# Weights of two experts at once on VectorE, one dot later, in a PEER decoder step

## The chip, the core and the metric

The kernel runs as one program on one core of a Trainium2 chip. The metric is the device time of one execution in microseconds (us). A core has these engines, each with an instruction stream of its own: TensorE (PE, its weight loads are listed as PEld), VectorE (DVE), ScalarE (ACT), GpSimd (POOL) and SyncE (SP), and 16 DMA engines that move data between HBM and the on-chip memory. Engines wait for each other by semaphores that the program counts up and waits on.

## The reference, cut to what matters

Two decoder layers for a prompt of 512 tokens and 8 sample tokens, in float32. Each layer has a token mixer (attention or a short convolution), a PEER expert layer and a small gated addition, with layer norms between. Nearly all of the time is PEER: for every token and each of 8 heads, the 16 best of 16,384 experts are found, and for each chosen expert one row of `u_tab` and one of `v_tab` (1,024 numbers each) are fetched.

```
def block(xt):                                  # 128 tokens
    ...
    top_s, top_p = lax.top_k(cand_s, PEER_TOPK)
    idx = jnp.take_along_axis(cand_i, top_p, axis=-1)
    g = jax.nn.softmax(top_s, axis=-1)          # gates: 128 x 8 x 16
    a = jnp.einsum('td,thkd->thk', xt, u_tab[idx])
    hk = (g * jax.nn.gelu(a, approximate=False)).astype(xt.dtype)
    return jnp.einsum('thk,thkd->td', hk, v_tab[idx])
```

So each expert of each token costs a dot of the token with its u row, a gelu of that dot, a product with the gate, and an addition of the v row weighted by that product.

## The kernel before, in words

Tokens lie on the 128 partitions. The prompt is four tiles of 128 tokens; the 8 sample tokens are a tile of their own. For a prompt tile there are 8 heads x 16 experts = 128 gathers; the sample tile's 8 x 128 expert rows are 8 gathers. A gather is one indirect DMA: POOL gives 128 indices, and each partition receives the 8 KB of its expert, u and v side by side. Both layers together have 1,040 gathers of 1 MB. They land in a ring of slots in the tile `arena`: 9 slots for the first 27 gathers, 11 afterwards.

What is done with a gather, in the order in which a slot passes it (experts are handled in pairs, `q` = 0 to 3 in a group of 8):

1. POOL issues the gather (line 989) when the slot has been released by the semaphore `slot_done`.
2. VectorE forms the dot in one instruction (line 1628, in `two_dots`), first of one expert, then of the other.
3. ScalarE does `two_experts` (line 1150): the gelu of the two dots (1154), a drain, two small products gelu x gate (1157, a copy with the gate as scale, 128x1 each), a drain, and the two row weightings (1164): the v row is scaled in place by its weight, 128x1024 each.
4. TensorE adds the weighted v rows to the accumulator `acc` in PSUM (1870 for prompt tiles, 1867 for the sample tile) and counts up `slot_done`.

The gates of a group of 8 are copied next to the gelus before its first pair (1190 for prompt tiles, 1193 for the sample tile). The last 8 experts of the program are not weighted row by row: ScalarE writes a diagonal matrix of the weights (1168), and TensorE multiplies the v rows by it (1855, the last pair 1842). Ahead of those, the accumulated sum is turned over: ScalarE copies `acc` to `yb` once (1172), and TensorE reads it back in (1833).

All other work (routing of the next tile, projections, norms) is cut into background pieces. A plan spreads them over the steps, one step a pair of experts. At step t TensorE does the pieces of step t; ScalarE and VectorE do the same pieces two steps later (`BEHIND = 2`). On both engines a step is first the background pieces, then the pair. Everything is written out in order in the program, so each engine works through a fixed list.

Of the kernel before, what the change touches and what calls it, by code (L numbers as in the profile page):

```python
# [25 lines left out]
P = 128  # L26
# [560 lines left out]
def build(nc, h0, h0T, consts, panels, ple_rows, keysT, uv0, uv1, cache_k, cache_v, pages, wlam, subg, ln, convw,  # L587
# [3 lines left out]
    with ctx:  # L591
        def sb(name, shape, dt=F32):
            return ctx.enter_context(nc.sbuf_tensor(name, shape, dt))
# [35 lines left out]
        act_w = sb("act_w", [P, 3, 2, GROUP])  # L629
# [161 lines left out]
        g_done = sem("gates_ready")  # L791
# [229 lines left out]
        def _(act):  # L1021
# [128 lines left out]
            def two_experts(G, q):  # L1150

                half, s = G % 2, slice(2 * q, 2 * q + 2)
                act.wait_ge(dot_done, G * GROUP + 2 * q + 2)
                nc.scalar.activation(act_w[:, 1, half, s], dots[:, half, s], ACT.Gelu).then_inc(gelu_done, 1)  # L1154
                act.drain()  # L1155
                for r in range(2 * q, 2 * q + 2):
                    nc.scalar.activation(act_w[:, 2, half, r:r + 1], act_w[:, 1, half, r:r + 1], ACT.Copy,  # L1157
                                         scale=act_w[:, 0, half, r:r + 1])
                act.drain()  # L1159
                for r in range(2 * q, 2 * q + 2):  # L1160
                    e = G * GROUP + r
                    if e < FIRST_BY_ROWS:
                        row = uv[:, slot_of(e), D:2 * D]
                        nc.scalar.activation(row, row, ACT.Copy, scale=act_w[:, 2, half, r:r + 1]).then_inc(weighted, 1)  # L1164
                        continue
                    if e >= FIRST_BY_ROWS + DIAGS:
                        act.wait_ge(slot_done, e - DIAGS + 1)
                    nc.scalar.activation(diag[:, r % DIAGS, :], const("ident"), ACT.Copy,
                                         scale=act_w[:, 2, half, r:r + 1]).then_inc(weighted, 1)
                if G * GROUP + 2 * q == FIRST_BY_ROWS:  # L1170
                    act.wait_ge(slot_done, FIRST_BY_ROWS)
                    nc.scalar.activation(yb[:], acc[:], ACT.Copy).then_inc(turned_over, 1)

            gates5 = gate[:].rearrange("p b h (a r) -> p b h a r", a=2)
            later = []
            for kind, layer, b, lots in steps:
# [6 lines left out]
                for t, G, q, hd, lot in window_pairs(layer, b, lots):  # L1183
# [4 lines left out]
                    if q == 0 and b < TB:  # L1188
                        act.wait_ge(g_done, place(layer, b) * HEADS + hd + 1)
                        nc.scalar.activation(act_w[:, 0, G % 2, :], gates5[:, b, hd, t // 4 % 2, :], ACT.Copy)  # L1190
                    elif q == 0:
                        act.wait_ge(ixs_ready, layer + 1)
                        nc.scalar.activation(act_w[:, 0, G % 2, :], gs8, ACT.Copy)
                    two_experts(G, q)
# [18 lines left out]
        def _(dve):  # L1213
# [307 lines left out]
            def gates(b, hd, unit):  # L1521
# [4 lines left out]
                V.tensor_scalar(gate[:, b, hd, :], r_ex, r_inv, None, ALU.mult).then_inc(g_done, 1)  # L1526
# [95 lines left out]
            def two_dots(G, q, x_rows):  # L1622
                for r in range(2 * q, 2 * q + 2):
                    e = G * GROUP + r
                    dve.wait_ge(gathered[slot_of(e)], 16 * (use_of(e) + 1))
                    if r == 0:
                        dve.wait_ge(gelu_done, G * 4 + 4)
                    V.tensor_tensor_reduce(uv[:, slot_of(e), 0:D], uv[:, slot_of(e), 0:D], x_rows, 1.0, 0.0, ALU.mult, ALU.add,  # L1628
                                           dots[:, G % 2, r:r + 1]).then_inc(dot_done, 1)

            later = []
            for kind, layer, b, lots in steps:
# [6 lines left out]
                for t, G, q, hd, lot in window_pairs(layer, b, lots):  # L1639
# [6 lines left out]
                    two_dots(G, q, h[:, b, :] if b < TB else x_sample[:])  # L1646
# [419 lines left out]
```

## Time and profile before

| | us |
|---|---|
| median of 3 runs | 3227.34 |
| lowest, highest | 3224.31, 3230.1 |
| the profiled execution, its own time | 3227.89 |
| its span in the profile | 3226.0 |
| TensorE busy | 2468.8 (77%) |
| VectorE busy | 2265.2 (70%) |
| ScalarE busy | 2039.5 (63%) |
| POOL busy | 1216.8 (38%) |
| mean DMA rate | 384 GB/s |

The span is the time between the first and the last instruction of the profiled execution; its own time is 1.89 us more. Busy shares are averages over the span. The first 330 us are the first layer's mixer; gathers run from then to the end. The page cuts the span in 40 slices; in nearly all of those behind the first five the 16 DMA engines are busy 90% or more. The granted TensorE clock is on average 0.875 of full speed.

### The profile page before, as it was taken

The numbers are of one execution on the slowest core, as the hardware profiler recorded it, in microseconds if no ns is written. First come the engines' busy times: TensorE is split into PE (matmuls) and PEld (weight loads), VectorE is DVE, ScalarE is ACT, GpSimd is POOL, SyncE is SP. The second block draws the span as 40 slices with busy tenths as digits, with TensorE's granted clock in tenths as the row PEclk, the third lists the DMA queues.
The fourth block names the chain that finished last, engine by engine and source line by source line (L and its number), as shares of the span: only waits on it lengthen the run. The fifth ranks groups of instructions, "written<-read, shape, count | busy, mean of one in ns | idle before, by whom it ended". The sixth has DMA issues, their size and how long they took to land.

```text
span 3226.0 us, 42783 instructions
## 1 busy us (share of the span) xinstructions
PE 2468.8 (77%) x13942; PEld 2068.6 (64%) x13942; DVE 2265.2 (70%) x5832; ACT 2039.5 (63%) x3623; POOL 1216.8 (38%) x1100
## 2 busy tenths in 40 slices
PE   9998777767756768777676987888788565687777
PEld 7766676657655657666665866676576554576665
DVE  0664677777688878776767667667667888669655
ACT  0143556676667876566756796556666676668983
POOL 0100444444444433334434444334443354434441
PEclk9998889989877889898898798999899777767899
DMA  4523999999999999999999899999999999989997
GB/s 182 209 105 133 359 408 420 421 403 422 418 421 421 407 418 421 421 419 420 419 415 412 343 421 421 421 421 421 420 417 421 411 412 421 421 337 421 421 421 297
DMA packets 178158, 1237.18 MB, mean 384 GB/s; under 512 B 19918, under 2 KB 23758, under 8 KB 31632
## 3 DMA queue, kind: packets, MB, share of 16 engines
q0 software_dynamic: 156896, 1115.93, 84.1%
q1 hardware_dynamic: 20896, 117.47, 9.1%
q8 instruction: 111, 1.82, 0.2%
q10 hardware_dynamic: 144, 1.05, 0.1%
q14 instruction: 111, 0.91, 0.1%
HBM read 1227.91 MB, written 6.50 MB: 383 GB/s over the span
## 4 chain that ended last, share of the span: by engine, by line
DMA 42%; PE 25%; DVE 14%; ACT 11%; issue 3%; DVEq 2%; ACTq 2%; POOL 1%; SPq 0%
DMA arena<-in_uv,idx 42%; DVE arena L1628 8%; PE acc L1870 7%; ACT arena L1164 6%; PE bank L1897 5%; PE bank L1671 4%; PE bank L1888 2%; PE bank L1718 2%; PE acc L1867 2%; ACT act_w L1157 1%; ACT L1154 1%; ACT L1148 1%; DVEq L1533 1%; ACTq L1155 1%; ACTq L1159 1%
## 5 line engine op out<-in xcount | busy, mean ns | idle before, releaser
L989 POOL DMA_INDIRECT arena<-in_uv,idx x1024 | 1166.2, 1139 | 1656.2 <-PE acc L1870 1420.8
L1870 PE MATMUL acc<-cst,arena 128*128 128x128 f32 x8128 | 1248.4, 315 | 678.6 <-ACT arena L1164 672.4
L1870 PEld LDWEIGHTS acc<-cst,arena 128*128 128x128 f32 x8128 | 1093.4, 164 | 848.4 <-ACT arena L1164 817.4
L1628 DVE CUSTOM_DVE_ANT_0 arena<-arena,h 128x1024 f32<-128x1024 f32 x1024 | 1231.8, 1222 | 496.6 <-DMA arena<-in_uv,idx 470.7
L1164 ACT ACTIVATE arena<-arena,act_w 128x1024 f32<-128x1024 f32 x1032 | 1130.3, 1142 | 37.2 <-issue 2.1
L1154 ACT ACTIVATE act_w<-dots 128x2 f32<-128x2 f32 x520 | 105.6, 203 | 755.8 <-DVE dots L1628 752.6
L1897 PE MATMUL bank<-hT,panel 128*128 128x264 f32 (+2 forms) x1760 | 413.3, 390 | 3.6 <-DMA panel<-in_panels 1.3
L1897 PEld LDWEIGHTS bank<-hT,panel 128*128 128x128 f32 x1760 | 334.5, 198 | 55.5 <-issue 6.2
L1157 ACT ACTIVATE act_w<-act_w 128x1 f32<-128x1 f32 x1040 | 250.2, 287 | 43.2 <-issue 1.1
L1154 ACT ACT_TABLE_LOAD x130 | 166.8, 1283 | 2.0 <-issue 0.2
L1888 PE MATMUL bank<-panel,qT 128*128 128x256 f32 (+1 forms) x640 | 152.6, 394 | 0.0
L1888 PEld LDWEIGHTS bank<-panel,qT 128*128 128x128 f32 (+1 forms) x640 | 112.0, 181 | 30.0 <-issue 2.8
L1888 PE MATMUL bank<-panel,hT 128*128 128x256 f32 (+1 forms) x448 | 104.0, 386 | 0.0
L1148 ACT ACT_TABLE_LOAD x80 | 102.6, 1283 | 1.4
L1888 PEld LDWEIGHTS bank<-panel,hT 128*128 128x128 f32 (+1 forms) x448 | 71.2, 164 | 24.8 <-issue 4.3
L1628 DVE DVE_READ_ACCUMULATOR2_ANT dots<- 128x1 f32 x1040 | 86.1, 83 | 0.0
L1033 ACT ACTIVATE qT<-bank 128x520 f32<-128x520 f32 x16 | 9.7, 604 | 111.9 <-PE bank L1671 111.9
L1462 DVE COPY yb<-tp 128x256 f32<-128x256 f32 x80 | 33.6, 420 | 55.8 <-PE tp L1818 54.6
L1064 ACT ACTIVATE arena<-arena,small 128x128 f32<-128x128 f32 (+3 forms) x64 | 35.5, 556 | 49.6 <-DVE small L1317 49.5
L1671 PE MATMUL bank<-keys,panel 128*128 128x256 f32 x256 | 60.2, 390 | 6.8 <-DMA panel<-in_panels 6.8
L1507 DVE TENSOR_TENSOR yb<-ya,cst 128x512 f32<-128x512 f32 x80 | 55.5, 693 | 12.4 <-issue 1.1
L1818 PE MATMUL tp<-keys,qT 128*128 128x128 f32 (+1 forms) x320 | 57.0, 308 | 7.9 <-issue 7.3
(241 smaller groups left out, 2398.6 us busy)
## 6 DMA issues: line engine op xcount, KB each, us to landing
panel<-in_panels SPq DMA_DIRECT2D x94, 1024.0 KB
arena<-in_uv,idx POOLq DMA_INDIRECT x1024
arena<-in_cache_k POOLq DMA_DIRECT2D x16, 512.0 KB, 5.6
arena<-in_cache_v POOLq DMA_DIRECT2D x16, 512.0 KB, 5.0
arena<-in_panels SPq DMA_DIRECT2D x6, 1024.0 KB, 6.9
arena<-out_y_s POOLq DMA_DIRECT2D x8, 512.0 KB, 5.7
h<-in_h SPq DMA_DIRECT2D x1, 2048.0 KB
out_nv_p<-arena POOLq DMA_DIRECT2D x4, 512.0 KB, 2.9
```

What stands on the lines that cost most here:

```text
L989: nc.gpsimd.indirect_dma_start(uv[:, slot_of(e), :], None, uv_dram[layer], bass.IndirectOffsetOnAxis(ids[:, r:r + 1], 0)).then_inc(gathere ...
L1148: nc.scalar.activation(r_ex, r_tv, ACT.Exp, bias=r_nm, accum_out=r_sum).then_inc(gexp_done, 1)
L1154: nc.scalar.activation(act_w[:, 1, half, s], dots[:, half, s], ACT.Gelu).then_inc(gelu_done, 1)
L1157: nc.scalar.activation(act_w[:, 2, half, r:r + 1], act_w[:, 1, half, r:r + 1], ACT.Copy, scale=act_w[:, 0, half, r:r + 1])
L1164: nc.scalar.activation(row, row, ACT.Copy, scale=act_w[:, 2, half, r:r + 1]).then_inc(weighted, 1)
L1628: V.tensor_tensor_reduce(uv[:, slot_of(e), 0:D], uv[:, slot_of(e), 0:D], x_rows, 1.0, 0.0, ALU.mult, ALU.add, dots[:, G % 2, r:r + 1]).the ...
L1671: m = mm(pj[n % 2][:, PW + G_OFF[g]:PW + G_OFF[g] + G_W[g]], w[:, c, :], src[g][:, c, 0:G_W[g]], start=(c == 0), stop=(c == C - 1))
L1718: t = mm(product_of[0:m, 0:PW], src[group_of(x.b)][:, c, local(x.b):local(x.b) + m], w[:, c, :], start=(c == 0), stop=(c == C - 1))
L1867: m = mm(acc[:, c * P:c * P + NS], row, const("group_of")[:, 0:NS], start=False, stop=True, skip_group_check=True)
L1870: m = mm(acc[:, c * P:(c + 1) * P], row, const("ident"), is_transpose=True, start=False, stop=True, skip_group_check=True)
L1888: last = mm(bank[0:m, x.n % BANKS, 0:PW], src[:, c, local(x.b):local(x.b) + m], weights[:, c, :], start=(c == 0), stop=(c == chunks - 1))
L1897: last = mm(bank[:, x.n % BANKS, 0:width], w[:, c, :], hT[:, c, lo:lo + width], start=(c == 0), stop=(c == C - 1))
```

## The change: who forms the weights, and when

ScalarE's `two_experts` is split in two. `two_gelus` does the gelu only and `two_rows` the two row weightings. The product gelu x gate is formed by VectorE, for two experts with one instruction (`two_weights`, a 128x2 tensor_tensor), straight from the tile `gate`. ScalarE's 1,040 single products, the 130 copies of gates and the two drains of each pair are gone. VectorE does the product of pair t-1 after the first dot of pair t. ScalarE's step is now: background pieces of the step, `two_rows` of the pair before, `two_gelus` of this pair. After a tile's last step, the last pair's product and rows follow directly. The semaphore that told ScalarE of the gates is replaced by one, `gated`, that counts products.

```
-            def two_experts(G, q):
+            def two_gelus(G, q):
                 half, s = G % 2, slice(2 * q, 2 * q + 2)
                 act.wait_ge(dot_done, G * GROUP + 2 * q + 2)
-                nc.scalar.activation(act_w[:, 1, half, s], dots[:, half, s], ACT.Gelu).then_inc(gelu_done, 1)
-                act.drain()
-                for r in range(2 * q, 2 * q + 2):
-                    nc.scalar.activation(act_w[:, 2, half, r:r + 1], act_w[:, 1, half, r:r + 1], ACT.Copy,
-                                         scale=act_w[:, 0, half, r:r + 1])
-                act.drain()
+                nc.scalar.activation(act_w[:, 0, half, s], dots[:, half, s], ACT.Gelu).then_inc(gelu_done, 1)
+
+            def two_rows(G, q):
+                half = G % 2
+                act.wait_ge(gated, G * 4 + q + 1)
                 for r in range(2 * q, 2 * q + 2):
...
@@ ScalarE's step
                         for x in later.pop(0):
                             background(x)
-                    if q == 0 and b < TB:
-                        act.wait_ge(g_done, place(layer, b) * HEADS + hd + 1)
-                        nc.scalar.activation(act_w[:, 0, G % 2, :], gates5[:, b, hd, t // 4 % 2, :], ACT.Copy)
-                    elif q == 0:
-                        act.wait_ge(ixs_ready, layer + 1)
-                        nc.scalar.activation(act_w[:, 0, G % 2, :], gs8, ACT.Copy)
-                    two_experts(G, q)
+                    if t > 0:
+                        two_rows(first_group(layer, b) + (t - 1) // 4, (t - 1) % 4)
+                    two_gelus(G, q)
+                two_rows(G, q)
...
@@ VectorE
+            def two_weights(layer, b, t):
+                G, q = first_group(layer, b) + t // 4, t % 4
+                s = slice(2 * q, 2 * q + 2)
+                dve.wait_ge(gelu_done, SEED_GELU + G * 4 + q + 1)
+                of = gate[:, b, t // 8, t % 8 * 2:t % 8 * 2 + 2] if b < TB else gs8[:, s]
+                V.tensor_tensor(act_w[:, 1, G % 2, s], act_w[:, 0, G % 2, s], of, ALU.mult).then_inc(gated, 1)
...
-                    two_dots(G, q, h[:, b, :] if b < TB else x_sample[:])
+                    x_rows = h[:, b, :] if b < TB else x_sample[:]
+                    dot(G * GROUP + 2 * q, x_rows)
+                    if t > 0:
+                        two_weights(layer, b, t - 1)
+                    dot(G * GROUP + 2 * q + 1, x_rows)
+                two_weights(layer, b, t)
```

VectorE, two steps in the middle of a tile, before. `ISA` is the dot (with the instruction behind it that reads out the sum), the rest are background pieces of the routing.

```order
L1628 ISA arena,dots<-arena,h 128x1024 [waits gathered1]
L1628 ISA dots 128x1
L1628 ISA arena,dots<-arena,h 128x1024 [waits gathered2]
L1628 ISA dots 128x1
L1476 MAX ya<-yb 128x8 x2
```

The same place after.

```order
L1624 ISA arena,dots<-arena,h 128x1024 [waits gathered1]
L1624 ISA dots 128x1
L1633 TENSOR_TENSOR act_w<-act_w,gate 128x2 [waits gelu_done]
L1624 ISA arena,dots<-arena,h 128x1024 [waits gathered2]
L1624 ISA dots 128x1
L1472 MAX ya<-yb 128x8 x2
```

Between the two dots of a pair there is now a product that waits for ScalarE's gelu of the pair before.

ScalarE, steps three and four of the first tile, before. `L1092` and `L1037` are background pieces (they square and spread the sample rows).

```order
L1154 ACTIVATE act_w<-dots 128x2 [waits dots_done]
L1157 ACTIVATE act_w<-act_w 128x1 x2
L1164 ACTIVATE arena<-arena,act_w 128x1024 x2
L1092 ACTIVATE arena<-bank 128x8x4 [waits bank_full]
L1037 ACTIVATE hT<-arena 128x2x132 x4
L1037 ACTIVATE x_sample<-arena 128x264 x3
L1037 ACTIVATE z<-arena 128x264
L1154 ACTIVATE act_w<-dots 128x2 [waits dots_done]
```

The same place after.

```order
L1154 ACTIVATE act_w<-dots 128x2 [waits dots_done]
L1092 ACTIVATE arena<-bank 128x8x4 [waits bank_full]
L1037 ACTIVATE hT<-arena 128x2x132 x4
L1037 ACTIVATE x_sample<-arena 128x264 x3
L1037 ACTIVATE z<-arena 128x264
L1164 ACTIVATE arena<-arena,act_w 128x1024 [waits weights_of_two_experts_ready]
L1164 ACTIVATE arena<-arena,act_w 128x1024
L1154 ACTIVATE act_w<-dots 128x2 [waits dots_done]
```

The row weightings of a pair have moved behind the next step's background pieces.

ScalarE at the end of the program, around the first pair of the last 8 experts, before.

```order
L1154 ACTIVATE act_w<-dots 128x2 [waits dots_done]
L1157 ACTIVATE act_w<-act_w 128x1 x2
L1168 ACTIVATE diag<-cst,act_w 128x128 x2
L1172 ACTIVATE yb<-acc 128x1024 [waits slots_done]
L1154 ACTIVATE act_w<-dots 128x2 [waits dots_done]
```

The same place after.

```order
L1154 ACTIVATE act_w<-dots 128x2 [waits dots_done]
L1168 ACTIVATE diag<-cst,act_w 128x128 [waits weights_of_two_experts_ready]
L1168 ACTIVATE diag<-cst,act_w 128x128
L1172 ACTIVATE yb<-acc 128x1024 [waits slots_done]
L1154 ACTIVATE act_w<-dots 128x2 [waits dots_done]
```

The diagonals, and with them the copy of `acc` behind them, now wait for a product that stands behind the first dot of the following pair.

## Rows read from the trace of the kernel before

**Rows 1.** Busy time by stretch: engines, PEclk, DMA share, GB/s.
```profile
core 0: us, PE busy (x) PEld busy (x) DVE busy (x) ACT busy (x) POOL busy (x), PEclk, DMA share, GB/s
328.00:500.00 172.00, 133.50 (x813) 116.13 (x812) 116.64 (x301) 104.78 (x195) 71.47 (x63) 0.88 0.96 389
...
1000.00:1500.00 500.00, 376.77 (x2222) 327.17 (x2223) 387.05 (x1038) 343.65 (x581) 195.82 (x176) 0.89 1.01 418
...
2780.00:2900.00 120.00, 91.28 (x468) 80.22 (x468) 81.76 (x204) 74.11 (x130) 45.32 (x40) 0.67 0.91 365
...
3170.00:3226.00 56.00, 46.06 (x162) 28.41 (x160) 23.27 (x43) 15.52 (x37) 0.94 (x1) 0.91 0.62 242
```
**Rows 2.** Waits: engine, line <- releaser: us in total, times, longest.
```profile
POOL arena L989 <- PE acc L1870: 1441.3, 574, 13.1
...
DVE arena L1628 <- DMA arena<-in_uv,idx: 470.7, 386, 3.8
```
**Rows 3.** Issue to landing: chain pieces (start, us, what), and a load of 512 KB.
```profile
339.73 9.45 DMA arena<-in_uv,idx
...
2779.05 20.02 DMA arena<-in_uv,idx
...
arena<-in_cache_k POOLq DMA_DIRECT2D x16, 512.0 KB, 5.6
```
**Rows 4.** VectorE in order of time, a steady stretch: start, us, [idle before <-releaser].
```profile
1525.36 1.23 DVE L1628 CUSTOM_DVE_ANT_0 arena<-arena,h 128x1024 f32<-128x1024 f32 x1 [1.25 <-DMA arena<-in_uv,idx]
```
**Rows 5.** VectorE in order of time, 2502 to 2520.
```profile
2508.73 1.23 DVE L1628 CUSTOM_DVE_ANT_0 arena<-arena,h 128x1024 f32<-128x1024 f32 x1 [0.37 <-DMA arena<-in_uv,idx]
...
2512.18 1.23 DVE L1628 CUSTOM_DVE_ANT_0 arena<-arena,h 128x1024 f32<-128x1024 f32 x1 [2.22 <-DMA arena<-in_uv,idx]
```
**Rows 6.** Instruction queue, packets, MB, share: whole span, then 1523:1524, then 2509:2510.
```profile
q14 instruction: 111, 0.91, 0.1%
...
q14 instruction: 1, 0.01, 1.9%
...
q14 instruction: 1, 0.01, 2.0%
```
**Rows 7.** Small VectorE instructions, groups by line: busy, mean ns, idle before.
```profile
L1499 DVE TENSOR_SCALAR ya<-ya 128x16 uint32<-128x16 uint32 x80 | 14.4, 180 | 6.1
L1495 DVE TENSOR_SCALAR ya<-ya 128x1 f32<-128x1 f32 x80 | 10.8, 135 | 0.0
```
**Rows 8.** ScalarE's products, the page's group.
```profile
L1157 ACT ACTIVATE act_w<-act_w 128x1 f32<-128x1 f32 x1040 | 250.2, 287 | 43.2 <-issue 1.1
```
**Rows 9.** ScalarE in order of time in the first tile.
```profile
350.47 0.20 ACT L1154 ACTIVATE act_w<-dots 128x2 f32<-128x2 f32 x1 [1.95 <-DVE dots L1628]
...
351.31 2.19 ACT L1164 ACTIVATE arena<-arena,act_w 128x1024 f32<-128x1024 f32 x2
```
**Rows 10.** Busy time by stretch at the start (columns as rows 1).
```profile
390.00:400.00 10.00, 9.27 (x38) 7.26 (x37) 3.64 (x7) 2.81 (x7) 0.70 (x1) 0.66 0.65 264
...
340.00:440.00 100.00, 74.11 (x448) 64.66 (x448) 61.85 (x140) 64.79 (x119) 39.08 (x35) 0.85 0.95 380
```
**Rows 11.** The two sample tiles: chain, then ScalarE and TensorE in order of time.
```profile
1774.06 25.66 PE acc L1867 x128
...
2844.58 1.06 ACT L1122 ACTIVATE h<-bank 128x512 f32<-128x512 f32 x2
...
2845.21 2.07 PE L1932 MATMUL bank<-lng,cst 8*128 8x512 f32 x2 [1.25 <-ACT h L1122]
```
**Rows 12.** The end: all engines in order of time, then the chain's last add.
```profile
3178.65 1.23 DVE L1628 CUSTOM_DVE_ANT_0 arena<-arena,h 128x1024 f32<-128x1024 f32 x1 [0.23 <-DMA arena<-in_uv,idx]
3178.88 1.00 ACT L1172 ACTIVATE yb<-acc 128x1024 f32<-128x1024 f32 x1
...
3179.93 1.10 PE L1833 MATMUL acc<-cst,yb 128*128 128x128 f32 x8
...
3197.07 3.65 PE acc L1842 x8
```

More of the change, by code:

```diff
@@ L628, in build @@
         dots = sb("dots", [P, 2, GROUP])
-        act_w = sb("act_w", [P, 3, 2, GROUP])
+        act_w = sb("act_w", [P, 2, 2, GROUP])
         small = sb("small", [P, 64])
@@ L790, in build @@
         idx_done = sem("expert_ids")
-        g_done = sem("gates_ready")
+        gated = sem("weights_of_two_experts_ready")
         gathered = [sem(f"gathered{r}") for r in range(SLOTS_UV)]
@@ L1163, in two_experts @@
                         row = uv[:, slot_of(e), D:2 * D]
-                        nc.scalar.activation(row, row, ACT.Copy, scale=act_w[:, 2, half, r:r + 1]).then_inc(weighted, 1)
+                        nc.scalar.activation(row, row, ACT.Copy, scale=act_w[:, 1, half, r:r + 1]).then_inc(weighted, 1)
                         continue
@@ L1168, in two_experts @@
                     nc.scalar.activation(diag[:, r % DIAGS, :], const("ident"), ACT.Copy,
-                                         scale=act_w[:, 2, half, r:r + 1]).then_inc(weighted, 1)
+                                         scale=act_w[:, 1, half, r:r + 1]).then_inc(weighted, 1)
                 if G * GROUP + 2 * q == FIRST_BY_ROWS:
@@ L1172, in two_experts @@
                     nc.scalar.activation(yb[:], acc[:], ACT.Copy).then_inc(turned_over, 1)
-            gates5 = gate[:].rearrange("p b h (a r) -> p b h a r", a=2)
             later = []
@@ L1525, in gates @@
                 dve.drain()
-                V.tensor_scalar(gate[:, b, hd, :], r_ex, r_inv, None, ALU.mult).then_inc(g_done, 1)
+                V.tensor_scalar(gate[:, b, hd, :], r_ex, r_inv, None, ALU.mult)
             def background(x):
@@ L1620, in background, with dot @@
                             gates(x.b, x.hd, x.u)
[L1622 to L1629, printed above, removed]
+            def dot(e, x_rows):
+                G, r = e // GROUP, e % GROUP
+                dve.wait_ge(gathered[slot_of(e)], 16 * (use_of(e) + 1))
+                if r == 0:
+                    dve.wait_ge(gelu_done, G * 4 + 4)
+                V.tensor_tensor_reduce(uv[:, slot_of(e), 0:D], uv[:, slot_of(e), 0:D], x_rows, 1.0, 0.0, ALU.mult, ALU.add,
+                                       dots[:, G % 2, r:r + 1]).then_inc(dot_done, 1)
+            def two_weights(layer, b, t):
[4 more added lines that the diff above has]
+                V.tensor_tensor(act_w[:, 1, G % 2, s], act_w[:, 0, G % 2, s], of, ALU.mult).then_inc(gated, 1)
             later = []
```

## The prediction

> **What bounds the kernel now.** I first read busy time by stretch [rows 1]. From about 330 us on the DMA share stands at 1.01 and the rate at 418 GB/s; it is lower only in the first 110 us of gathering (0.96 over 328 to 500), around the sample tile of the second layer (0.91) and at the end (0.62). No engine is as full: in 1000 to 1500 VectorE has 387 of 500 us, TensorE 377, ScalarE 344. So over some 2,800 us the transfer of expert rows sets the pace, and the engines only have to keep up.
>
> The waits say the same [rows 2]. VectorE's dots wait 470.7 us for gathers to land. POOL waits 1441.3 us for a slot, but that wait costs nothing: a gather of 1 MB takes 2.49 us at the full rate (a dot of 1.23 us behind a wait of 1.25 us, again and again [rows 4]), yet from issue to landing it takes 20 us in the bulk, against 5.6 us for a load with nothing queued ahead of it [rows 3]. The difference, some 14 us, is time in the queue. A slot released 3 or 5 us later there makes its gather wait less in the queue and land at the same time. At the start the cushion is thin: 9.45 us to landing, so about 4 us.
>
> Then I looked for what makes a landing late although the queue is full. In 2502 to 2520 dots start at 2508.73 and 2512.18: 3.45 us apart instead of 2.49, with 2.22 us of waiting for the DMA [rows 5]. In 2509 to 2510 lies a packet of the queue q14, which fetches instructions [rows 6]. 0.91 MB in 111 packets is 8.2 kB each. I counted the trace's records: VectorE 8,109, ScalarE 4,742, POOL 1,341, SP 144, together 112 times 128, so one packet brings 128 instructions. Packets that come when VectorE has gone through a further 128 instructions are followed by such a gap, 8 of 8 times between 2509 and 2811 us. One that belongs to ScalarE, at 1523 us, leaves the pace at 2.48 us [rows 4, 6]. The reading: a gather is whole only when each of the 16 DMA engines has done its share, one of the 16 is always the last, and it is the one that also fetches for VectorE. Each such fetch costs the bound resource 3.45 - 2.49 = 0.96 us.
>
> The Trainium skill speaks against that (Runtime: NRT & Kernel Launch, Instruction fetch mechanics): blocks of 16 KiB are fetched by the sequencer's own DMA queue, a cost "mostly hidden". The trace has packets of 8.2 kB, and the gap behind VectorE's is there; by the page the first term below would be nothing. That is rival A.
>
> **The change part by part.** All terms are made against the profiled execution, 3227.89 us (span 3226.0 and 1.89 around it).
>
> *Removed from ScalarE.* 1,040 products at 287 ns by their rows, or 0.24 us each back to back, 250.2 us [rows 8], the gate copies and 1,040 drains. In the bulk ScalarE is 69% busy [rows 1] and beside the DMA, so this gives nothing there. ScalarE's program is 2,208 instructions shorter, 17 fetches, which by rows 4 and 6 lay on another DMA engine: nothing (if on the bound one, -16 us: rival D).
>
> *Added to VectorE: busy time.* No 128x2 tensor_tensor stands in this trace. The nearest rows are 135 ns for 128x1 and 180 ns for 128x16 [rows 7]; up to the 287 ns of ScalarE's product it could be. At 150 ns, 520 of them are 78 us. They lie within the 470.7 us that VectorE waits for gathers [rows 2]: 0. Were that cover gone (as it is where background pieces crowd), it would be 0.15 us a pair. The product's wait for the gelu is for a pair whose dots ended at least one landing (2.49 us) earlier; the gelu takes 0.20 us, so it is normally long done. It isn't if ScalarE is behind, in two row weightings (2.19 us) and a background piece; behind the product then stand the second dot and all background pieces of VectorE, and behind these TensorE's routing work. In the bulk that is within 14 us of cushion.
>
> *Added to VectorE: instructions.* 520 more are 520/128 = 4.06 fetches at 0.96 us: +3.9. Bounds 0 (hidden) and +3.9.
>
> *Moved: the release of slots.* The rows of a pair are weighted after the next pair's first dot and ScalarE's next background piece, so 2.5 to some 6 us later. In the bulk hidden by the cushion [rows 3]: 0. Four places have little or none.
>
> The start, 340 to 440 us. The DMA share is 0.95 there, against 1.01: 5.9 us of idle DMA, most in 390 to 400 (0.65) [rows 10]; over 328 to 500 it is 0.96, 8.5 us [rows 1]. Two effects oppose each other. From gelu to rows there are 0.84 us (350.47 to 351.31), of which only the gelu's 0.20 and the switch stay [rows 9], so each pair takes ScalarE 0.6 us less where it is nearly full, and its background pieces, which feed the next tile's routing, come before the rows. Against that the slots come free later, with 4 us of cushion. The bounds are -5.9 (all of the idle recovered) and +4 (the 6 us of a late release less the gain of three pairs); I take -2, nearer to the relief, since it acts on every pair and the delay only on those behind a long piece.
>
> The first layer's sample tile, about 1774 us: TensorE is busy without a break for 25.66 us with 128 small adds [rows 11], and that sets the dip. It starts when ScalarE's first rows are done, at most 0.7 us later or earlier: 0.
>
> The second layer's, about 2845 us: TensorE waits 1.25 us for ScalarE's copy `L1122`, which stands behind two row weightings of 2.19 us [rows 11]. Now the copy is a background piece ahead of them, but the last pair of the tile before waits about 1 us longer for its product. Between -1.5 and +1, I take -0.5.
>
> The end. The products of experts 1032 and 1033 now wait for the dot of 1034, which starts at 3178.65 and ends at 3179.88. Then come the product with its signal (0.3), the two diagonals (0.69 us together) and the copy of `acc` (1.00), which before started at 3178.88 [rows 12]. So the copy ends about 3181.9 and TensorE's 1833, at 3179.93 before, starts at about 3181.95. From there to 3200.7 TensorE has no break (the adds, with projections between, up to the last at 3197.07, 3.65 us [rows 12]), while the last gather's dot ends at about 3192.3. So the whole is late: +2.0 (bounds 0, if the planned pieces in between give, and +2.5).
>
> **Sum.** +3.9 - 2.0 - 0.5 + 2.0 = +3.4 us on 3227.89: 3231.3. The median of the runs is 0.55 us below the profiled one, so 3230.7, in round figures 3231.
>
> **The rivals.**
> A: VectorE's fetches cost nothing more (the queue absorbs them, or the last of the 16 DMA engines isn't the one). For: fetches that ScalarE makes show no gap. Against: the gap of 0.96 us behind VectorE's. The sum is then -0.5: 3227.4 - 0.5, about 3227.
> B, slower by more: the loop at the start. A pair's product waits for the landing of the next pair's first gather, so a slot's release now depends on a gather issued later. With 9 slots and 4 us of cushion [rows 3], each pair behind a long ScalarE or VectorE piece holds back two slots, and the idle of 340 to 440 grows by as much again: +5.9 where I took -2, so 3231 + 8 = 3239. It decides as soon as releases come over 4 us later. For it: the share dips to 0.65 already [rows 10]. Against: 64.79 us busy of 100 for ScalarE and 61.85 for VectorE, so a delay is caught up.
> C, faster: the relief of ScalarE at the start wins back the idle by all of 8.5 us [rows 1]: 3231 - 6.5 = 3224 to 3225; with fetches hidden too, 3221.
> D: ScalarE's 17 fetches do lie on the bound DMA engine: -16 beside the rest, with 0.96 us apiece, and the tail's +2.0: 3211 to 3215. The row at 1523 speaks against it. That the change doesn't do what it says is excluded by the order of instructions.
>
> **How the numbers follow.** What a measurement of this kernel can tell from no change is 0.2%, 6.5 us: below 3220.9 is faster, above 3233.8 slower. The forecast of +3.4 has 0.43, with 3227 to 3235 as its own range: 0.31 of it is no change, 0.12 slower. A has 0.22: 0.21 no change, 0.01 faster. B has 0.22: 0.18 slower, 0.04 no change. C has 0.10, one half faster and one half no change. D has 0.03, faster. Together faster 0.09, same 0.61, slower 0.30. The range reaches from C's 3222 to a bit beyond B, 3243 (a second tile's start hit by the same loop).
>
> **What the profile after would show.** If the steps are right: the bulk keeps DMA share 1.01 and 417 to 421 GB/s, but each stretch of 500 us has nearly one VectorE fetch more, and the gaps of about 3.45 us between dots stand behind these; the dots in mid-program come 1 to 3 us later than before against their place at 500 us. The product takes 0.13 to 0.18 us and its waits are mostly absent. In 340 to 440 the DMA share is 0.96 or 0.97. TensorE's 1833 starts 3.2 us behind the dot of expert 1034, instead of 1.3. The forecast is wrong if the share in 340 to 440 falls under 0.93 (B), if the last dots come no later than before relative to the start though 4 fetches were added (A), or if ScalarE's rows are waited for by VectorE in the bulk.

## The result and the profile after

The kernel after takes 3233.03 us (median of 17 runs, 3228.45 to 3236.11), the one before in the same sessions 3227.73 (17 runs). The ratio is 1.0015, with a 95% interval of 1.0008 to 1.0021: some 4.8 us slower (2.6 to 6.8), where +3.4 was forecast. The profiled execution has a span of 3230.8 us, 4.8 more than before.

Busy time by stretch in the profile after (columns as in [rows 1]); the last row is beside [rows 10].

```profile
328.00:500.00 172.00, 134.52 (x799) 114.03 (x798) 119.30 (x329) 88.67 (x130) 73.17 (x63) 0.86 0.95 384
...
1000.00:1500.00 500.00, 383.35 (x2208) 335.92 (x2207) 392.46 (x1123) 294.19 (x382) 209.28 (x177) 0.87 1.00 413
...
2780.00:2900.00 120.00, 90.60 (x482) 78.73 (x480) 84.60 (x225) 63.49 (x84) 46.70 (x43) 0.73 0.96 382
...
3170.00:3226.00 56.00, 47.10 (x184) 28.92 (x185) 26.34 (x53) 15.95 (x29) 4.03 (x4) 0.97 0.66 264
...
340.00:440.00 100.00, 75.84 (x445) 64.32 (x438) 63.04 (x151) 54.05 (x80) 39.95 (x35) 0.81 0.92 368
```

ScalarE is 49 us of 500 less busy in mid-program (294 against 344) and nothing comes of it: the DMA share stays at 1.00 to 1.01. In 340 to 440 the share fell from 0.95 to 0.92 where a rise to 0.96 or 0.97 was forecast; that is under the 0.93 which the prediction had named as a sign of rival B. Around the second sample tile it rose from 0.91 to 0.96.

The waits after (engine, line, releaser: us in total, times, longest).

```profile
POOL arena L989 <- PE acc L1879: 1426.1, 612, 12.1
ACT arena L1164 <- DVE act_w L1633: 975.5, 460, 6.7
...
DVE arena L1624 <- DMA arena<-in_uv,idx: 435.0, 358, 4.0
```

ScalarE's idle time moved from the gelus to the rows: its wait for dots is now a wait for products. VectorE waits 435.0 us for gathers, 36 less than in [rows 2], since the products fill part of it. The product itself, from the page's groups:

```profile
L1633 DVE TENSOR_TENSOR act_w<-act_w,gate 128x2 f32<-128x2 f32 x512 | 80.1, 156 | 53.7 <-ACT act_w L1154 51.1
```

156 ns each, between the bounds of [rows 7], and 51.1 us of waiting for gelus in all.

VectorE's dots in a steady stretch, and the instruction packet in 2475 to 2476.

```profile
2473.36 1.22 DVE L1624 CUSTOM_DVE_ANT_0 arena<-arena,h 128x1024 f32<-128x1024 f32 x1
...
2475.66 1.23 DVE L1624 CUSTOM_DVE_ANT_0 arena<-arena,h 128x1024 f32<-128x1024 f32 x1 [1.07 <-DMA arena<-in_uv,idx]
...
2476.81 0.16 DVE L1633 TENSOR_TENSOR act_w<-act_w,gate 128x2 f32<-128x2 f32 x1
...
2479.11 1.22 DVE L1624 CUSTOM_DVE_ANT_0 arena<-arena,h 128x1024 f32<-128x1024 f32 x1 [2.14 <-DMA arena<-in_uv,idx]
```
```profile
q14 instruction: 1, 0.01, 2.0%
```

As in [rows 5], the dot behind a VectorE fetch comes 3.45 us after the one ahead of it, not 2.49. I took the landing of each gather from the trace and looked, between 500 and 2780 us, at the landings around each q14 packet. Before, 31 of 52 packets of VectorE's have a gap of 3.35 to 3.55 us beside them and 0 of 31 others; after, 33 of 56 and 0 of 16. (Most of VectorE's remaining ones meet a longer gap; that a panel of weights lands in it is not shown for each.)

A gather counts as landed when the last of 16 signals has come. The trace of the kernel `tail` below, which has after's instructions and nearly all of these signals, shows which of them is late. At 36 gaps of 3.35 to 3.55 us beside VectorE's packets the last signal comes 3.45 us behind the last one of the gather before, while each of the other 15 keeps a distance of 2.48 or 2.49 us (medians by rank; in 11 of the 36 some earlier one slipped too). Between gathers 200 and 500 the last signal is 8.3 us behind the one before it (median). So what paces the landings, and what a fetch for VectorE puts off, is one share of 16. That is the prediction's reading; which DMA engine a signal belongs to the trace doesn't say.

**Where the 4.8 us are.** The same landings give the place. The figures are how much later a gather lands than in the profile of before.

| landing of gather | after, minus before |
|---|---|
| 0 (nothing changed ran yet: scatter) | +0.9 |
| 60 (511 us) | +3.1 |
| 914 (2857 us) | +6.4 |
| 926 (2900 us) | +2.2 |
| 1039, the last (3191 us) | +3.8 |
| end of span | +4.8 |

So: +0.9 ahead of the first gather, +2.2 at the start, +3.3 over the bulk, -4.2 at the second sample tile, +1.6 in the last tile, +1.0 at the end. This is one pair of profiles; in those of all 14 kernels the first gather lands between 331.8 and 337.2 us.

The end, all engines in order of time, and the chain's last add (beside [rows 12]).

```profile
3182.45 1.23 DVE L1624 CUSTOM_DVE_ANT_0 arena<-arena,h 128x1024 f32<-128x1024 f32 x1 [0.24 <-DMA arena<-in_uv,idx]
...
3184.39 1.00 ACT L1172 ACTIVATE yb<-acc 128x1024 f32<-128x1024 f32 x1
...
3185.45 1.09 PE L1842 MATMUL acc<-cst,yb 128*128 128x128 f32 x8 [0.89 <-ACT yb L1172]
```
```profile
3202.57 3.65 PE acc L1851 x8
```

The turn back (1842, before 1833) starts 3.00 us behind the dot of expert 1034; before it was 1.28. The 1.7 us stay to the last add, which starts 7.7 us behind the last dot's start instead of 6.1.

TensorE around the second sample tile, after.

```profile
2842.74 2.05 PE L1835 MATMUL acc<-cst,h 128*128 128x128 f32 x16 [1.53 <-ACT lnb L1204]
...
2847.95 1.39 PE L1941 MATMUL bank<-lng,cst 8*128 8x512 f32 x2 [0.38 <-ACT h L1122]
...
2849.28 7.00 PE L1876 MATMUL acc<-cst,arena 128*128 128x8 f32 x32
```

The wait for `L1122` fell from 1.25 us [rows 11] to 0.38. The 16 turning products in front took 2.05 us, before 3.78 (the line of before stands below): the granted clock in 2836 to 2846 is 1.00 here (2.4 GHz throughout) and 0.67 there, as the same stretch of after and of before shows (busy time of TensorE, PEclk, DMA share, GB/s):

```profile
2836.00:2846.00 10.00, 7.53 (x57) 1.00 1.01 420
```
```profile
2836.00:2846.00 10.00, 7.64 (x31) 0.67 0.89 370
```
```profile
2837.40 3.78 PE L1826 MATMUL acc<-cst,h 128*128 128x128 f32 x16 [1.11 <-ACT lnb L1208]
```

The change is not what raised the clock: three kernels below that keep before's order (`v_drains`, `v_signals`, `both_signals`) have these 16 products in 2.05 us as well.

### The profile page after: what moved, and what is told of

Same layout as the page of the kernel before. It is cut to its first block, busy times and chain, and to the rows that moved or that the text cites. A ratio compares the mean times of both kernels' runs of the same rounds, so it can differ in the third digit from the quotient of the medians.

```text
span 3230.8 us, 41095 instructions
## 1 busy us (share of the span) xinstructions
PE 2488.0 (77%) x13942; PEld 2085.1 (65%) x13942; DVE 2304.5 (71%) x6352; ACT 1752.8 (54%) x2453; POOL 1254.7 (39%) x1100
## 4 chain that ended last, share of the span: by engine, by line
DMA 41%; PE 25%; DVE 20%; ACT 6%; DVEq 4%; issue 3%; POOL 1%; SPq 0%; ACTq 0%
DMA arena<-in_uv,idx 40%; DVE arena L1624 9%; PE acc L1879 7%; ACT arena L1164 4%; PE bank L1906 4%; PE bank L1680 4%; PE bank L1897 3%; PE bank L1727 2%; PE acc L1876 1%; DVEq L1529 1%; DMA arena<-in_uv,small 1%; POOL arena L989 1%; DVE ya L1487 1%; DVE ya L1475 1%; PE bank L1732 1%
## 5 line engine op out<-in xcount | busy, mean ns | idle before, releaser
L989 POOL DMA_INDIRECT arena<-in_uv,idx x1024 | 1205.7, 1177 | 1619.2 <-PE acc L1879 1401.3
L1879 PE MATMUL acc<-cst,arena 128*128 128x128 f32 x8128 | 1263.0, 318 | 688.9 <-ACT arena L1164 686.6
L1624 DVE CUSTOM_DVE_ANT_0 arena<-arena,h 128x1024 f32<-128x1024 f32 x1024 | 1247.3, 1221 | 446.3 <-DMA arena<-in_uv,idx 435.0
L1906 PE MATMUL bank<-hT,panel 128*128 128x264 f32 (+2 forms) x1760 | 424.5, 397 | 1.9 <-DMA panel<-in_panels 1.2
L1906 PEld LDWEIGHTS bank<-hT,panel 128*128 128x128 f32 x1760 | 343.7, 204 | 56.0 <-issue 3.3
L1633 DVE TENSOR_TENSOR act_w<-act_w,gate 128x2 f32<-128x2 f32 x512 | 80.1, 156 | 53.7 <-ACT act_w L1154 51.1
L1509 DVE TENSOR_TENSOR yb<-yb,ya 128x512 f32<-128x512 f32 x80 | 55.5, 693 | 6.7 <-issue 0.9
L1680 PE MATMUL bank<-hT,panel 128*128 128x264 f32 x256 | 59.6, 386 | 0.0
```

Source lines behind the costliest of these rows:

```text
L989: nc.gpsimd.indirect_dma_start(uv[:, slot_of(e), :], None, uv_dram[layer], bass.IndirectOffsetOnAxis(ids[:, r:r + 1], 0)).then_inc(gathere ...
L1633: V.tensor_tensor(act_w[:, 1, G % 2, s], act_w[:, 0, G % 2, s], of, ALU.mult).then_inc(gated, 1)
L1680: m = mm(pj[n % 2][:, PW + G_OFF[g]:PW + G_OFF[g] + G_W[g]], w[:, c, :], src[g][:, c, 0:G_W[g]], start=(c == 0), stop=(c == C - 1))
L1879: m = mm(acc[:, c * P:(c + 1) * P], row, const("ident"), is_transpose=True, start=False, stop=True, skip_group_check=True)
L1906: last = mm(bank[:, x.n % BANKS, 0:width], w[:, c, :], hT[:, c, lo:lo + width], start=(c == 0), stop=(c == C - 1))
```

## The experiments

Each kernel was timed against the kernel before on the same chip; ratios are with 95% intervals. "Landing" is taken as in the table above. Comparisons with after go through these ratios, as both were timed against before. `...` marks where an edit is cut.

**1. More instructions on VectorE.** Kernel `v_drains`, against before:

```
     ... dots[:, G % 2, r:r + 1]).then_inc(dot_done, 1)
+                for _ in range(4):
+                    dve.drain()
```

> The kernel before with 4 further drains on VectorE behind the second dot of each pair: 2,080 instructions more on VectorE, nothing else changed. Theory (a fetch for VectorE holds back the landings by 0.96 us per 128 instructions): 16.25 fetches, +15.6 us, and 16 more gaps of about 3.45 us between landings. Rival A (fetches are hidden, only the time that VectorE is busy could matter, and it waits 471 us for gathers): within 2 us of before.

Measured: 3242.5 us, ratio 1.0044 (1.0030 to 1.0058), +14.2 us. The instruction queue's row, over the whole span:

```profile
q14 instruction: 128, 1.05, 0.1%
```

17 packets more than in [rows 6], and from gather 60 to 900 the landings lose 14.8 us, spread evenly (+4.5 at gather 200, +7.5 at 400, +12.0 at 600, +16.1 at 900). The start is as before. So rival A is out: 0.87 us a fetch by the median. The 16 further gaps of about 3.45 us did not all show as such: between 500 and 2780 us there are 69 packets of VectorE's instead of 52, and 39 instead of 31 with such a gap; more than before meet a longer one.

**2. The same on ScalarE.** Kernel `s_drains`:

```
                     two_experts(G, q)
+                    for _ in range(4):
+                        act.drain()
```

> The kernel before with 4 further drains on ScalarE behind each pair: 2,080 instructions more on ScalarE. Theory (ScalarE's fetches go by another DMA engine than the bound one): within 2 us of before, though q14 fetches 16 packets more. Rival D (any fetch holds back the landings): +15.6 us.

Measured: 3233.91 us, 1.0015 (1.0006 to 1.0024), +4.8 us. Neither theory in full. The landings tell it apart: from gather 0 to 60 it loses 3.2 us, and from 60 to 900 0.3 us, with 16 packets more; 1 of 38 packets that aren't VectorE's has a gap of 3.45 us. ScalarE's fetches cost next to nothing. Its time at the start costs up to 3 us; kernels that leave ScalarE's order there as before scatter from -0.3 to +2.4 us in that stretch (experiment 11), so how much is open. The stretch in `s_drains`:

```profile
340.00:440.00 100.00, 76.02 (x427) 66.39 (x428) 60.70 (x133) 64.90 (x117) 39.26 (x34) 0.80 0.91 367
```

**3. Fewer instructions on VectorE.** Kernel `v_signals`, against before: a small class around VectorE's calls turns each drain into a wait. The core of it:

```
    def drain(self):
        ...
        if self.last is not None and self.last.signal is None:
            self.last.then_inc(self.chain, 1)        # the instruction ahead signals
        ...
        self.pending = self.last.signal              # the next one waits for it
```

> The kernel before with VectorE's drains replaced, wherever the instruction ahead can signal, by a wait of the next instruction on a semaphore of VectorE's own: 1,647 instructions fewer on VectorE, 12.9 fetches. All else stands in the same order. Theory: -12.4 us, 3215. Rival A: within 2 us of before, or slower by what the signals take longer than drains.

Measured: 3214.39 us, 0.9956 (0.9942 to 0.9969), -14.2 us.

```profile
q14 instruction: 98, 0.80, 0.1%
```

13 packets fewer, 1.10 us apiece. From gather 60 to 900 the landings gain 15.6 us. The kernel's order is that of before, so the gain needs no change of order to explain it. That signals are also quicker than drains can't be excluded for some of the 1.8 us above the forecast. Beside VectorE's packets between 500 and 2780 us there are some 27 gaps of about 3.45 us, where before has 31. Around the second sample tile TensorE waits longer for the copy `L1122` (line 1184 here) than the 1.25 us of [rows 11]:

```profile
2832.37 2.01 PE L1994 MATMUL bank<-lng,cst 8*128 8x512 f32 x2 [2.98 <-ACT h L1184]
```

**4. Rows and products first.** Kernel `rows_first`, against after:

```
@@ ScalarE's step; VectorE's in the same way
+                    if t > 0:
+                        two_rows(first_group(layer, b) + (t - 1) // 4, (t - 1) % 4)
                     if len(later) > BEHIND:
                         for x in later.pop(0):
                             background(x)
-                    if t > 0:
-                        two_rows(first_group(layer, b) + (t - 1) // 4, (t - 1) % 4)
                     two_gelus(G, q)
```

> The kernel after, with the product of pair t-1 moved to the head of VectorE's step t (ahead of its background pieces) and ScalarE's rows of pair t-1 ahead of its background pieces. The 520 products stay. Theory (fetches cost 3.9 us; at the start the late release costs 2 us, at the end the late product 1 to 2 us): before + 3 us or less, that is 2 to 3 us below after. Rival A (the fetches cost nothing and the whole loss of after is the late release): before - 1 to 0.

Measured: 3238.43 us, 1.0029 (1.0020 to 1.0038), +9.4: a miss, slower than after. Its waits, first of VectorE's product, then of ScalarE:

```profile
DVE act_w L1633 <- ACT act_w L1154: 261.0, 520, 18.9
...
ACT arena L1164 <- DVE act_w L1633: 118.2, 516, 0.3
```

At the head of a step the product meets a gelu that is only being made: VectorE waits 261.0 us in 520 waits, against 54.0 in 36 waits in after (same view). I had counted the earlier release as pure gain and left out VectorE's wait with the background pieces behind it. By the landings it loses 0.8 us from gather 0 to 60 and 5.0 from 60 to 900 (after 2.2 and 2.1). At the second sample tile `L1122` is again behind the rows:

```profile
2854.08 2.07 PE L1941 MATMUL bank<-lng,cst 8*128 8x512 f32 x2 [2.30 <-ACT h L1122]
```

**5. The order without the products.** Kernel `copies_late`, against after:

```
             def two_rows(...):
...
-                act.wait_ge(gated, G * 4 + q + 1)
+                act.drain()
+                act.wait_ge(dot_done, seen)          # the first dot of the next pair
+                for r in range(2 * q, 2 * q + 2):
+                    nc.scalar.activation(act_w[:, 1, half, r:r + 1], act_w[:, 0, half, r:r + 1], ACT.Copy, scale=of)
+                act.drain()
@@ VectorE
-                    if t > 0:
-                        two_weights(layer, b, t - 1)
...
-                two_weights(layer, b, t)
```

> The order of the kernel after (rows of a pair behind the next pair's first dot and the next background pieces on ScalarE), but the products stay on ScalarE (1,040 scaled copies and both drains a pair); VectorE's program is as long as before. It tells the 520 instructions from the order. Theory (4 fetches of VectorE's cost 3.9 us): 4 us below after, that is before + 0 to 2. Rival A (the instructions are free and the order is what costs): like after, before + 5; and as ScalarE has no relief here it could be above that.

Measured: 3231.88 us, 1.0007 (0.9998 to 1.0016). Alone this doesn't separate it from after. By the landings it loses 5.6 us from gather 0 to 60 (after 2.2) and gains 1.9 from 60 to 900 (after loses 2.1). So in the same order the products cost 4.0 us over 840 gathers, for which 3.3 fetches at 0.96 us would be 3.1; and without the relief of ScalarE the late order costs 3.4 us more at the start. Its profile is of its slowest run (3236.63 us), so the end of it is not compared.

**6. The end.** Kernel `tail`, against after:

```
                     two_gelus(G, q)
+                    if G * GROUP + 2 * q == FIRST_BY_ROWS:
+                        two_rows(G, q)
@@ VectorE, behind the second dot
+                    if G * GROUP + 2 * q == FIRST_BY_ROWS:
+                        two_weights(layer, b, t)
... and both are left out at that pair's usual place
```

> The kernel after with one pair changed, that of experts 1032 and 1033: its product stands directly behind its own second dot, and its diagonals and the copy of acc ahead of the next gelus. Theory: from the last landing to the end 34.6 us instead of 36.0, the time 1 to 2 us below after. Rival (TensorE's planned pieces give, and the tail is set by the last pair): no change. Up to gather 1032 it is a second look at after's curve of landings.

Measured: 3231.85 us, 1.0013 (1.0004 to 1.0022): 0.6 to 1.2 us below after, less than the two can tell apart. From the last landing to the end of the span it takes 35.5 us (after 36.0, before 35.0), where 34.6 were expected. TensorE's adds with diagonals in that kernel:

```profile
3182.37 1.04 PE L1846 MATMUL acc<-cst,yb 128*128 128x128 f32 x8
3183.24 3.60 PE L1868 MATMUL acc<-arena,diag 128*128 128x512 f32 x8
...
3187.19 3.70 PE L1868 MATMUL acc<-arena,diag 128*128 128x512 f32 x8 [0.35 <-ACT diag L1168]
```

The turn back came earlier, but the next pair's diagonals are still one dot late, and TensorE now waits for those. The last add starts 7.3 us behind the start of the last dot (7.7 in after, 6.1 before). Its landings repeat after's: +1.9 us from gather 0 to 60, +2.2 from 60 to 900.

**7. Two pairs late.** Kernel `two_late`, against after, on both engines:

```
-                    if t > 0:
-                        two_weights(layer, b, t - 1)
+                    if t > 1:
+                        two_weights(layer, b, t - 2)
...
```

> The kernel after with products and rows a further pair later (two pairs behind the dots). The instructions are the same, only the release of each slot is some 5 us later again. Theory (cushion of 14 us in the bulk, thin at the start, after the second sample tile and at the end): after + 4 to 7 us, of it 2 to 3 before the 60th gather and 2.5 at the end, nothing between 500 and 2780 us. Rival B (late releases cost everywhere): after + 15 or more, with the DMA share under 1.00 in the bulk.

Measured: 3760.32 us, 1.1639 (1.1616 to 1.1661). A miss by a hundred times. Its waits, and one turn of the loop from the chain of work between 1500 and 1520 us:

```profile
DVE yb L1459 <- PE tp L1829: 356.9, 76, 16.6
ACT qT L1129 <- PE bank L1908: 314.1, 67, 13.3
```
```profile
1502.74 0.08 DVE act_w L1634
...
1502.85 1.16 ACT arena L1164
...
1504.05 6.48 PE acc L1881 x32
1510.53 3.47 PE bank L1908 x16
...
1514.02 0.42 DVE qT L1573
```

What waits here are background pieces, for TensorE's half of them. TensorE's half stands behind its adds, the adds behind ScalarE's rows, the rows behind VectorE's product, and that product stands one step ahead of the piece that waits. Between 1500 and 1520 us no landing stands in the chain, and over the whole span landings hold 2.4% of it, against 42% in before: the ring of slots is not what slows this kernel.

**8. The same with a step more.** Kernel `two_late_behind3` is `two_late` with one line changed.

```
-BEHIND = 2
+BEHIND = 3
```

> two_late (products and rows two pairs behind the dots, 3760 us) with BEHIND = 3: VectorE and ScalarE do the background pieces of a step three steps after TensorE, instead of two. Theory: two_late was slow by a loop inside one step. VectorE's product at step s+1 frees ScalarE's rows (2.2 us), these TensorE's add (3.0) and the pieces behind it (3.6), and VectorE's own pieces at step s+2 wait for those: 9 us of chain in a step that may take 5. With BEHIND = 3 the chain has a step more, as after has it with BEHIND = 2, and most of the 530 us go: 3235 to 3260. Rival (late release: the ring of slots is too short for it): the release is as late as in two_late, so the time stays above 3600.

Measured: 3258.8 us, 1.0097 (1.0081 to 1.0112); 500 of the 530 us are gone, though slots are released just as late. The first of the waits above is now

```profile
DVE yb L1459 <- PE tp L1829: 23.4, 5, 12.5
```

Between gather 100 and 400 its landings keep their distance to before (+9.4 and +8.7 us): a release two pairs late costs nothing there, which bears the cushion out for a steady stretch. It isn't free elsewhere: it loses 6.9 us from gather 0 to 60, 6.4 behind the first layer's sample tile (gather 520 to 560, where after loses 0.4), and from the last landing to the end it takes 42.2 us (after 36.0).

**9. After with a step more.** Kernel `after_behind3` is after with the same line.

> The kernel after with BEHIND = 3, nothing else. Theory: in after the same loop has two steps (some 10 us) for 9 us of chain and does not bind in the bulk, so this gives nothing: after within 3 us. Rival (the loop already costs after part of its loss, at the start or behind the sample tile): 2 to 5 us below after.

Measured: 3244.4 us (3237.05 to 3246.9), 1.0050 (1.0036 to 1.0064), some 11 us above after: slower than both theories had it. Its profile is of its fastest run, and there the bulk is as in after (+2.2 from gather 60 to 900), so the loop does not bind in after. From gather 914 to 926 it takes 44.6 us, after 38.1, and there the place is plain: `L1122` stands a step later on ScalarE, behind two more row weightings that wait for their product, and TensorE waits for it.

```profile
2851.25 2.07 PE L1941 MATMUL bank<-lng,cst 8*128 8x512 f32 x2 [5.63 <-ACT h L1122]
```

In after that wait is 0.38 us; the 5.25 us more cover the 4.4 that lie between the two profiled executions. What adds up to 10 us more in its slower runs stays open.

**10. After with signals.** Kernel `after_signals` is after with the class of `v_signals`.

> The kernel after with VectorE's drains replaced by waits on semaphores of its own as in v_signals: 1,650 instructions fewer on VectorE. Theory: after - 13 us (12.9 fetches at 0.96 to 1.1), 3220, and 5 us above v_signals. Rival A (v_signals was faster because a drain takes longer than a signal, at places where VectorE sets the pace): since VectorE here has more to do, the same gain or more, and no relation to the fetches; the landings would show it by gaps of 3.45 us as many as in after.

Measured: 3219.19 us, 0.9968 (0.9956 to 0.9980), which by the ratios is 15 us below after for 12.9 fetches (the page shows 11 packets fewer), and 3.9 us (by the ratios) above `v_signals`. From gather 60 to 900 its landings gain 11.1 us on after's. Rival A had as many gaps of 3.45 us as in after; beside VectorE's packets there are some 26 between 500 and 2780 us, against 33.

**11. First tile as before.** Kernel `first_tile_before`, against after:

```
+                if G < 16:
+                    act.drain()
+                    for r in range(2 * q, 2 * q + 2):
+                        ...   # ScalarE's scaled copies from the gate tile
+                    act.drain()
+                else:
+                    act.wait_ge(gated, G * 4 + q + 1 - 64)
...
```

> The kernel after, but the first tile (pairs 0 to 63) in the order of the kernel before, with the products on ScalarE directly behind the gelus; 64 products fewer on VectorE. It tests the term for the start. Theory (relief of ScalarE and late release nearly cancel at the start: 1 us lost): 0 to 2 us below after, and the 60th gather lands 0 to 3.3 us later than in the profile of before, as it does in the other kernels with that order. Rival (my forecast of a gain of 2 us at the start): 2 us above after.

Measured: 3230.46 us, 1.0008 (0.9999 to 1.0017), some 2 us below after, though the intervals overlap. From gather 0 to 60 it loses 0.0 us, as `v_drains` (-0.3) does, where after, `tail`, `after_signals` and `after_behind3` lose 2.2, 1.9, 2.5 and 1.8. Of the kernels with before's order `v_signals` (2.4) doesn't fit and `both_signals` (1.4) lies between. So in this stretch the late order gains nothing, and its loss is 1 to 2 us. The DMA share in 340 to 440 says the same: 0.93 to 0.95 in the five kernels with before's order and ScalarE's drains not added to, 0.91 to 0.93 in the four with after's.

**12. The best version.** Kernel `both_signals` is `v_signals` with ScalarE's drains replaced too and the copies of gates dropped.

```
                 nc.scalar.activation(act_w[:, 1, half, s], dots[:, half, s], ACT.Gelu).then_inc(gelu_done, 1)
-                act.drain()
...
+                act.wait_ge(gelu_done, SEED_GELU + G * 4 + q + 1)
...
```

> v_signals (the kernel before with VectorE's drains as signals, 3214) with ScalarE's two drains a pair replaced in the same way and the copies of gates dropped (the products on ScalarE read the gate tile). Theory: no fetch of VectorE's more or less; ScalarE has some 0.3 us a pair less where it is nearly full, which at the start gives back 1 to 3 us, as 4 drains more cost 3 to 5 there: 3211 to 3214. Rival (ScalarE's time is hidden throughout): same as v_signals within 1 us.

Measured: 3211.13 us, 0.9946 (0.9933 to 0.9960), 17 us below before and 22 below after. Against `v_signals` it is 3.3 us faster by the medians; the intervals of the two overlap. In the two profiles all of that lies ahead of the first gather, which lands at 331.8 us here and at 335.1 there; from that landing to the last one it takes 2.4 us more. So the runs don't show that ScalarE's relief gave anything.

## Why the prediction was right, step by step

The forecast was 3231 us, +3.4; measured were 3233.03 and +4.8 (2.6 to 6.8). The bulk's term was right for the reason given. The rest of the sum held by luck: the start was off by +4.2 us and the second sample tile by -3.7, and the two cancel; the last tile's 1.6 and the 0.9 us of scatter ahead of the first gather had no term, and the end came out at half its term.

- *The bulk is set by landings, ScalarE's relief gives nothing there.* Right: ScalarE lost 49 us of busy time in 500, and the DMA share stayed. One stretch was passed over when the places with less than the full share were named: around the first layer's sample tile (1740 to 1860 us) the profile of before has 0.92, that of after 0.93.
- *520 instructions on VectorE, 4.06 fetches, +3.9.* Right, and the term best supported: +14.2 us for 16.25 fetches more, -14.2 for 12.9 fewer. That is 0.87 to 1.10 us a fetch, against 0.96 forecast. In the landings of after the bulk lost 3.3 us, by the comparison with `copies_late` 4.0. The Trainium skill (Runtime: NRT & Kernel Launch, Instruction fetch mechanics) calls the cost of crossing a block, one bump of a DMA queue's tail, mostly hidden. For ScalarE's fetches the runs agree (0.3 us from gather 60 to 900 with 16 packets more in the program), for VectorE's they don't, and the measurement decides.
- *ScalarE's fetches lie on another DMA engine (rival D excluded).* That they cost nothing is right by `s_drains`. VectorE's delay just the last of a gather's 16 signals; for ScalarE's no signal was found that is late more often than elsewhere, so that they lie on another DMA engine is the reading that fits, and not shown.
- *The product costs 135 to 285 ns, hidden.* 156 ns; hidden in the wait for gathers.
- *The start, -2.* Wrong in sign: +2.2 in this pair of profiles, 1 to 2 us by all kernels together, inside the bounds given (-5.9 to +4). The step took the relief as the greater because it acts on every pair, and called ScalarE nearly full there; by [rows 10] it is 65% busy in 340 to 440, less than the 69% of mid-program. Without the relief (`copies_late`) the late order costs 5.6 us, so by that one pair of profiles the relief was worth 3.4 and the delay 5.6. The share of 0.92 in 340 to 440 was to mean rival B, with 3239 us; it came with a time near the forecast, so that sign was set too close: kernels with before's order have 0.93 to 0.95 there.
- *The second sample tile, -0.5.* The mechanism was right and the size off, -4.2. From gather 914 to 926 the five kernels with before's order take 40.8 to 43.0 us, `rows_first` 43.1, the four with after's order and products 37.7 to 38.6, `copies_late` 40.6. `copies_late` has the late order without the products on VectorE and gains less, so both belong to it. What TensorE loses there is laid out in two places that stand for each other. In before the 16 turning products take 1.7 us more than in after, at the lower clock, and the wait for `L1122` is 1.25 us, together 3.0. In `v_drains` and `v_signals` these products run as fast as in after, and the wait is 2.98 us: the copy comes behind ScalarE's rows, whatever TensorE's clock. In all five with before's order the two come to 2.8 to 3.6 us, in those with the late order and `BEHIND = 2` to 0 to 0.4, in `after_behind3` to 5.6. So the copy's place is worth 2.6 us in this pair; the rest of the 4.2 isn't laid out. The bound of -1.5 came from the wait alone and didn't ask how much longer it is when TensorE is there sooner.
- *The end, +2.0.* +1.7 to the last add, and 0.7 of it came back behind it: +1.0 from the last landing to the end. The turn back starts 3.00 us behind the dot of expert 1034; the prediction's own sum gives 3.3, its list of signs 3.2.
- *The release of slots is hidden by 14 us of cushion.* Right for a steady stretch, by `two_late_behind3`.
- *Rival B.* The loop was real but described at the wrong place. I told of it as slots held back at the start. What binds in `two_late` is the loop of background pieces, VectorE to ScalarE to TensorE and back, over two steps in after and one in `two_late`. In after it does not bind in the bulk; one more pair of delay and it costs 530 us. I did not see it either when I wrote the expectation for `two_late`.
- The last tile's +1.6 us (gathers 926 to 1039) had no term of its own beyond its share of the fetches, half a microsecond; the rest is within what two profiles differ by.

## What to carry to other kernels

Where landings of a full DMA queue set the pace, count an engine's instructions and not only its busy time: a few hundred tiny instructions, or drains, can cost as much as they save elsewhere. Before delaying a product by a step, follow the chain through all engines back to the same engine, and compare its length with the steps that are left: here 9 us of chain fit into two steps of some 5 us and not into one. Relief on an engine with idle time gave nothing in the bulk; at the start, where slots have the least time to spare, it was worth 3.4 us by one pair of profiles.

## What the runs showed of the hardware

- Replacing drains on VectorE by waits attached to the next instruction took 1,647 instructions out and made the program 14.2 us faster (0.9956), though VectorE was 70% busy and waited 471 us for data.
- Beside 31 of 52 packets of VectorE's instructions the next landing comes 3.45 us behind the one before instead of 2.49, beside none of the 31 other packets in before and 1 of 38 in `s_drains`. In `tail` only the last of a gather's 16 signals is late at such gaps (3.45 us, the other 15 at 2.48 or 2.49).
- In the second sample tile 16 products took 3.78 us at a granted clock of 0.67 and 2.05 us at 1.00 (the clock as the mean over 10 us), with the engine's idle time ahead of them 1.11 and 1.53 us.
